# Decay rows through DRAM, one exponential for both masks, and squared norms of k from one-column products, in a hybrid decoder layer

## The reference

```python
kd = l2norm(heads(ck, DN_H))                       # k / sqrt(sum(k * k) + eps), per token and head
g = -jnp.exp(dn_a_log) * jax.nn.softplus(da + dn_dt_bias)
beta = jax.nn.sigmoid(db)
...
G = jnp.cumsum(gc, axis=-1)
diff = G[..., :, None] - G[..., None, :]
dec = jnp.where(incl, jnp.exp(jnp.where(incl, diff, 0.0)), 0.0)
kk = jnp.einsum('bhid,bhjd->bhij', kc, kc)
a_mat = jnp.where(strict, kk * dec * bc[..., :, None], 0.0)
eG = jnp.exp(G)[..., None]
...
qk = jnp.einsum('bhid,bhjd->bhij', qc, kc) * dec
```

## Time and profile before

| | us |
|---|---|
| median of 3 runs | 823.36 (823.05 to 825.56) |
| profiled execution, its time | 822.85 |
| its span in the profile | 821.0 |
| PE, busy | 802.8 |
| DVE, busy | 405.6 |
| ACT, busy | 214.8 |
| POOL, busy | 152.6 |

### The profile page before, as it was taken

One profiled execution on the slowest core, in us unless ns is written; L12 is line 12 of the kernel. 1 busy time (PEld: TensorE's weight loads), 2 busy tenths in 40 slices (PEclk: granted clock), 3 DMA queues, 4 the chain that ended last, 5 costly groups with the idle time before them and its releaser, 6 DMA issues. The chain is left out here.

```text
span 821.0 us, 12877 instructions
## 1 busy us (share of the span) xinstructions
PE 802.8 (98%) x5172; PEld 504.8 (61%) x5172; DVE 405.6 (49%) x886; ACT 214.8 (26%) x469; POOL 152.6 (19%) x182
## 2 busy tenths in 40 slices
PE   9999999999999999999999999999999999999995
PEld 4446777887889987777777776455433333334443
DVE  4223556684666522663853458826352101104976
ACT  3202152239324311131101110122121111125275
POOL 0324420004055223300220034000100001004100
PEclk9999999999999999999999999999999999999999
DMA  9521344503020200514241123134899999995211
GB/s 360 229 85 32 120 166 154 157 18 111 1 104 3 77 29 14 204 52 124 103 177 65 67 103 119 65 131 183 308 397 362 421 426 423 402 400 204 77 52 65
DMA packets 20977, 135.23 MB, mean 165 GB/s; under 512 B 2437, under 2 KB 3077, under 8 KB 13749
## 3 DMA queue, kind: packets, MB, share of 16 engines
q1 hardware_dynamic: 13328, 103.08, 32.1%
q0 software_dynamic: 4720, 23.83, 7.9%
q10 hardware_dynamic: 2868, 7.47, 3.0%
HBM read 118.94 MB, written 19.63 MB: 169 GB/s over the span
## 5 line engine op out<-in xcount | busy, mean ns | idle before, releaser
L818 PE MATMUL pair<-mem 128*128 128x288 f32 x640 | 158.9, 408 | 0.0
L818 PEld LDWEIGHTS pair<-mem 128*128 128x128 f32 x640 | 120.3, 190 | 35.6 <-ACT mem L1506 2.1
L986 PE MATMUL single<-mem 128*128 128x288 f32 x448 | 110.0, 407 | 0.2
L986 PEld LDWEIGHTS single<-mem 128*128 128x128 f32 x448 | 84.7, 190 | 25.7 <-issue 1.6
L1373 PE MATMUL single<-mem 128*32 128x512 f32 x768 | 85.1, 594 | 0.9 <-DVE mem L2539 0.9
L1506 ACT ACTIVATE mem<-pair 128x512 f32<-128x512 f32 (+5 forms) x83 | 36.5, 487 | 162.6 <-PE pair L818 63.1
L1506 ACT ACTIVATE mem<-single 128x256 f32<-128x256 f32 (+5 forms) x109 | 44.6, 419 | 126.9 <-PE single L1234 48.5
L2532 DVE SCALAR_TENSOR_TENSOR mem<-single,mem 128x256 f32<-128x256 f32 x12 | 5.8, 484 | 102.3 <-PE single L1373 91.4
L1373 PEld LDWEIGHTS single<-mem 128*32 128x32 f32 x768 | 23.6, 110 | 52.8 <-issue 51.7
L1225 PE MATMUL pair<-mem 128*128 128x512 f32 x112 | 51.0, 601 | 0.0
L1442 PE MATMUL pair<-mem 128*128 128x512 f32 x112 | 49.4, 595 | 0.3 <-DVE mem L2600 0.3
(11 more groups left out here) (431 smaller groups left out, 1118.1 us busy)
## 6 DMA issues: line engine op xcount, KB each, us to landing
mem<-in_w_gu SPq DMA_DIRECT2D x17, 2048.0 KB, 14.4
mem<-in_w_down SPq DMA_DIRECT2D x17, 1024.0 KB, 13.2
y_slots<-mem SPq DMA_DIRECT2D x9, 512.0 KB, 10.5
y_slots<-in_zeros POOLq DMA_DIRECT2D x8, 512.0 KB, 8.6
mem<-in_w_ga SPq DMA_DIRECT2D x2, 2048.0 KB, 7.7
mem<-in_w_gb SPq DMA_DIRECT2D x2, 2048.0 KB, 7.6
mem<-in_w_wo SPq DMA_DIRECT2D x2, 2048.0 KB, 7.7
mem<-in_w_pg SPq DMA_DIRECT2D x2, 2048.0 KB, 16.6
```

Source lines behind the costliest of these rows:

```text
L818: last = nc.tensor.matmul(pb[:, hf, 0:HALF], w(k), rhs[:, k, hf * HALF:(hf + 1) * HALF], start=(k == 0), stop=(k == kk - 1))
L986: last = nc.tensor.matmul(single[plan.buf[s]][:, 0:HALF], lhs[:, k, :], rhs[:, k, :], start=(k == 0 and j in (0, 1, 3, 4)), stop=(k == 3), ...
```

## The change

- `gG` is one step instead of five. PE makes the running sums of all tiles and heads as rows of 16 and of 4 partitions, with two products; DVE copies them to `grow`; ACT's queue writes them to DRAM (`g_rows`, two transfers).
- `gL`, new, after `nl` in block 6: ACT's queue reads each tile's four rows back to all 128 partitions (five transfers, into `Gr`).
- `gD` is gone. In `gE` ACT takes |G_j - G_i| with four absolute values (bias `gcum`, scale -1) into `D2`, one exponential with scale -1, and the one for `E`; POOL makes both masks out of `D2`, the one into `A` first. ACT waits for all five transfers before the first tile.
- `gs` is one step instead of five. POOL squares k in four products (`ksq`, in the buffers of `n_rows`, after the last `nf` and after the masks of tiles 0 and 1), PE multiplies tiles of the squares with one column of ones, DVE copies 20 columns out.
- The order: `gC` and `gG` from block 7 to block 4, ahead of `rN`; `gE` from blocks 9 and 10 to 7 (tiles 0, 1), 8, 9 and 10; `gs`, `gX` and `gr` in block 10.

```diff
     between = {2: [("nq", "rN", m) for m in (0, 1)], 3: [("nq", "rN", m) for m in (2, 3)],
-               4: [("rN",), ("nr", "rN")], 5: [("ns", "rN")], 6: [("nl", "rN")],
-               7: nf("rN", (0, 1)) + [("gC",), ("gG", 0), ("gG", 1), ("gD", 0), ("gD", 1)],
-               8: nf("rN", (2, 3)) + [("gG", t) for t in range(2, NT)] + [("gD", t) for t in range(2, NT)],
-               9: [("gs", t) for t in range(3)] + [("gE", 0), ("gE", 1)],
-               10: [("gs", 3), ("gs", 4)] + [("gE", t) for t in range(2, NT)] + [("gX",)], 11: [("gr",)]}
+               4: [("gC",), ("gG",), ("rN",), ("nr", "rN")], 5: [("ns", "rN")], 6: [("nl", "rN"), ("gL",)],
+               7: nf("rN", (0, 1)) + [("gE", 0), ("gE", 1)], 8: nf("rN", (2, 3)) + [("gE", 2)], 9: [("gE", 3)],
+               10: [("gs",), ("gE", 4), ("gX",), ("gr",)], 11: []}
...
+    g_rows = nc.dram_tensor("g_rows", (NT * H, P), F32, kind="Internal").ap()
...
-        ksq = [view(slot(14 + i), H, DK) for i in range(2)]
+        ksq = nrow["rN"]
...
                 elif k0 == "gG":
-                    t, n = s[1], ntok(s[1])
                     pe.wait_ge(sem("g_beta"), 1)
-                    out = heads(s, P, n)
-                    for h in range(H):
-                        last = nc.tensor.matmul(out[:, h, :], gl[0:n, t, h:h + 1].broadcast_to([n, P]), tri(t),
-                                                start=True, stop=True)
+                    out = single[plan.buf[s]]
+                    nc.tensor.matmul(out[0:16, 0:P], gl[:, 0:4, :], tri(0), start=True, stop=True)
+                    last = nc.tensor.matmul(out[32:32 + H, 0:64], gl[0:64, 4, :], tri(4), start=True, stop=True)
                     last.then_inc(s_mm, 1)
...
                 elif k0 == "gs":
-                    t, n = s[1], ntok(s[1])
-                    pe.wait_ge(sem("conv"), 8)
-                    out = single[plan.buf[s]][0:n, :].rearrange("p (h w) -> p h w", h=H)
-                    for h in range(H):
-                        last = nc.tensor.transpose(out[:, h, :], cs[:, 4 + h, t * P:t * P + n], C("ident"))
+                    pe.wait_ge(sem("ksq"), H)
+                    for t in range(NT):
+                        for h in range(H):
+                            at = H * t + h
+                            last = nc.tensor.matmul(single[plan.buf[s]][0:ntok(t), at:at + 1], ksq[h][:, t * P:t * P + ntok(t)],
+                                                    C("ones")[:, 0:1], start=True, stop=True)
                     last.then_inc(s_mm, 1)
...
-                elif k0 == "gs":
-                    t, n = s[1], ntok(s[1])
-                    mm_wait(act, s)
-                    if t >= 2:
-                        ev_wait(act, ("gs", t - 2))
-                    for h in range(H):
-                        last = nc.scalar.activation(ksq[t % 2][0:n, h, :], single[plan.buf[s]][0:n, h * DK:(h + 1) * DK], ACT.Square,
-                                                    accum_out=kr[0:n, 0, t, h:h + 1])
-                    last.then_inc(ev(k0), 1)
...
                 elif k0 == "gG":
-                    t, n = s[1], ntok(s[1])
-                    mm_wait(act, s)
+
+                    ev_wait(act, s)
+                    act.dma_start(g_rows[0:16, :], grow[0:16, :]).then_inc(sem("g_stored"), 16)
+                    act.dma_start(g_rows[16:20, 0:64], grow[32:36, 0:64]).then_inc(sem("g_stored"), 16)
+                elif k0 == "gL":
+
+                    act.wait_ge(sem("g_stored"), 32)
                     act.wait_ge(sem("ret_free"), 1)
-                    copy(Gr[t], heads(s, P, n)).then_inc(ev(k0), 1)
+                    for t in range(NT):
+                        n = ntok(t)
+                        act.dma_start(Gr[t], g_rows[4 * t:4 * t + 4, 0:n].unsqueeze(0).broadcast_to([P, H, n])).then_inc(sem("g_rows"), 16)
                 elif k0 == "gE":
                     t, n = s[1], ntok(s[1])
-                    act.wait_ge(sem("gdiff"), t + 1)
-                    nc.scalar.activation(A[t], A[t], ACT.Exp, scale=-1.0).then_inc(sem("gexp"), 1)
-                    nc.scalar.activation(D2[t], D2[t], ACT.Exp).then_inc(sem("gexp"), 1)
+                    ev_wait(act, ("gC",))
+                    act.wait_ge(sem("g_rows"), 16 * NT)
+                    for h in range(H):
+                        last = nc.scalar.activation(D2[t][:, h, :], Gr[t][0:n, h, :], ACT.Abs, bias=gcum[0:n, t, h:h + 1], scale=-1.0)
+                    link(last)
+                    nc.scalar.activation(D2[t], D2[t], ACT.Exp, scale=-1.0).then_inc(sem("gexp"), 1)
                     nc.scalar.activation(E[t], Gr[t], ACT.Exp).then_inc(sem("gexp"), 1)
...
-                elif k0 == "gD":
-                    t, n = s[1], ntok(s[1])
-                    ev_wait(dve, ("gG", t))
-                    for h in range(H):
-
-                        V.tensor_scalar(A[t][:, h, :], Gr[t][0:n, h, :], gcum[0:n, t, h:h + 1], 0.0, ALU.subtract, ALU.max)
-                        last = V.tensor_scalar(D2[t][:, h, :], Gr[t][0:n, h, :], gcum[0:n, t, h:h + 1], 0.0, ALU.subtract, ALU.min)
-                    last.then_inc(sem("gdiff"), 1)
+                elif k0 == "gG":
+                    mm_wait(dve, s)
+                    V.tensor_copy(grow[0:16, :], single[plan.buf[s]][0:16, 0:P])
+                    V.tensor_copy(grow[32:36, 0:64], single[plan.buf[s]][32:36, 0:64]).then_inc(ev(k0), 1)
+                elif k0 == "gs":
+                    mm_wait(dve, s)
+                    V.tensor_copy(kr[:, 0, 0:4], single[plan.buf[s]][:, 0:16].rearrange("p (t h) -> p t h", t=4))
+                    V.tensor_copy(kr[0:64, 0, 4], single[plan.buf[s]][0:64, 16:20]).then_inc(ev(k0), 1)
...
+                elif k0 == "nf" and s[1:] == ("rN", 3):
+
+                    pool.wait_ge(sem("nfin"), 4)
+                    for h in range(H):
+                        pool.wait_ge(sem("conv"), H + h + 1)
+                        G.tensor_tensor(ksq[h], cs[:, H + h, :], cs[:, H + h, :], ALU.mult).then_inc(sem("ksq"), 1)
                 elif k0 == "gE":
                     t, n = s[1], ntok(s[1])
                     if t == 0:
                         pool.wait_ge(sem("nfin"), 4)
                         G.memset(nwz, 0.0).then_inc(sem("zeroed"), 1)
-                    pool.wait_ge(sem("gexp"), 5 * t + 1)
-                    G.tensor_tensor(A[t], A[t], bh(C("low") if t < 4 else C("low_s", 64), n, n), ALU.mult).then_inc(sem("gmask"), 1)
-                    pool.wait_ge(sem("gexp"), 5 * t + 2)
+                    pool.wait_ge(sem("gexp"), 4 * t + 1)
+                    G.tensor_tensor(A[t], D2[t], bh(C("low") if t < 4 else C("low_s", 64), n, n), ALU.mult).then_inc(sem("gmask"), 1)
+                    pool.wait_ge(sem("gmask"), 2 * t + 1)
                     G.tensor_tensor(D2[t], D2[t], bh(tri(t), n, n), ALU.mult).then_inc(sem("gmask"), 1)
```

9 lines of the change are left out of this document (5 added, 4 removed).

## The result

| | before | after |
|---|---|---|
| median of 6 runs, us | 824.2 (822.82 to 825.94) | **836.24** (832.74 to 839.46) |
| ratio | | 1.0144, 95% interval 1.012 to 1.0168 |
| profiled execution, its time | 822.85 | 837.3 |
| its span | 821.0 | 835.5 |

The account below looks back on a forecast made before the run. PE was taken as the bound, busy 802.8 of 821.0 us. 822.85 + 4.1 (block 11 later) + 2.0 (clock) = 828.95; with the median 0.5 higher, 829.5 us, range 824 to 837.

Parts of the forecast that it names:

- PE's balance: PE's work in gG and gs: 6.98 us removed, 0.5 and 4.3 added, 2.2 us less.
- one column is nearly free: Rival on gs: its one-column products cost at most 1.0 us instead of 4.3, no difference in time; chance 0.03.
- Step 1, shift: On PE, gC and gG ahead of rN delay block 7 by 1.26 us; block 10 ends at 182.7.
- Step 2, arrival: The five g_rows transfers from DRAM have all landed at 167 us, between a floor of 162.9 and a ceiling of 170.9.
- w_dz goes first: Rival on the transfers: rows land at 172, with short pieces costing 1 us; about 835.5 us; chance 0.13.
- in time: Rival on the transfers: rows land by 161.7, result 822.2 us, not slower; chance 0.22 for in time or nearly.
- Step 3, ACT: On ACT, gE of tiles 0 and 1 takes 5.7 us after the rows arrive, before block 8's evacuation.
- Step 4, DVE: From block 8's evacuation through convolution and two nf to the release of POOL's memset: 5.96 us.
- Step 5, POOL: POOL's memset, four masks and four squares of k (ksq) ahead of gs take 10.45 us.
- The wait: PE, ready for gs at 182.7, stands 6.4 us until POOL's squares are done at 189.1.
- The clock: The granted clock may fall during PE's standing, slowing gs and part of block 11: 2.0 us taken, at most 12.
- the clock holds: Rival on PE's clock after its standing: no fall, 827.5 us; counted within the forecast's 0.57, without its own chance.

Follow-up runs that it names:

- e12: The changed kernel with rows of tiles 0 and 1 on their own semaphore and POOL squaring k ahead of memset and first masks; 823.78 us, ratio 0.9998 to before.
- e1: The changed kernel with the exponentials (gE) one block later in the order; 823.83 us, ratio 1.0011 to the kernel before.
- e4: The changed kernel with 16 useless products on PE ahead of gs's wait; 831.78 us, ratio 1.0101 to the kernel before.
- e13: e1 with 128 columns of ones in each product of squares instead of one; 822.56 us, ratio 0.9994 to the kernel before.
- e5: The changed kernel with POOL squaring k ahead of the memset and the masks of tiles 0 and 1; 829.18 us, ratio 1.0056 to the kernel before.
- e6: The changed kernel with ACT waiting for the transfers of tiles 0 and 1 alone, on their own semaphore; 831.44 us, ratio 1.009 to the kernel before.
- e9: e1 with 24 columns of ones in each product of squares instead of one; 824.52 us, ratio 1.0003 to the kernel before.
- e2: The kernel before with only the squares of k changed (POOL squares, PE's one-column products), decay rows as they were; 829.82 us, ratio 1.0062.
- e7: The changed kernel with gs and gr after block 11 instead of block 10; 825.28 us, ratio 1.0031 to the kernel before.
- e8: e1 with gs split, tiles 0 and 1 after block 10 and the rest after block 11; 823.9 us, ratio 0.9996 to the kernel before.
- e3: The changed kernel with the norms of k as before (transposes, ACT's Squares) and the exponentials late; 820.39 us, ratio 0.9966 to the kernel before.

## Why the prediction was right in direction and short in size

The mechanism came true: the rows hold ACT, ACT holds DVE, DVE holds POOL, and PE stands for POOL's squares. What failed are sizes in the sum: the term for the clock, 2.0, measured 5.35; the wait, 6.4, measured 8.56; and the pause of 1.44 behind had no term.

**One sum fits the runs with products of squares.** At full clock and without a wait the changed stretch is 71.14 - 4.80 - 2.18 + 0.53 + 4.11 = 68.80. Add each run's waits and half of the time that PE worked at half clock: e12 68.80 + 1.7 = 70.5 (70.49 measured), e1 + 3.4 = 72.2 (72.01), e4 + 7.76 + 1.7 = 78.3 (78.25), e13 + 0.57 = 69.4 (69.37), e5 + 3.81 + 5.1 = 77.7 (77.94), e6 + 4.44 + 6.05 = 79.3 (79.19), the change + 8.56 + 5.35 = 82.7 (82.69).

- *PE's balance*, -2.2: right. 68.80 against 71.14 is -2.3. The price of the one-column products, 4.3, taken from the weights of the nearest row, measured 4.11. The rival "one column is nearly free" is dead: 4.11/40 is 0.103 us a record. The floor of 25 ns that the Trainium skill states ("TensorE: Matmul & The Clock Gate", section "Wait — 56ns, not 53.3ns?") doesn't carry over to products that load new weights each. Here the weights set the pace: in e9 the 40 weight loads take 4.36 us, one behind the other, and 24 columns cost what one does (4.15 against 4.11).
- *Step 1, shift*: right. Block 10 ended at 184.92, less the late start 182.95, against 182.7.
- *Step 2, arrival*: 167 forecast; 169.72 - 1.97 = 167.75. Right, on the row taken as nearest; "w_dz goes first" (172) and "in time" (162) did not occur. The transfers landed 6.9 to 9.0 us after their issue. That it varies by 3.3 us from run to run wasn't in the forecast. It may be part of the changed kernel's spread (832.74 to 839.46); that isn't shown.
- *Step 3, ACT*: 5.7 forecast, 6.37 measured. Four absolute values take 1.3 us, not 0.8 and a 0.2 wait.
- *Step 4, DVE*: 5.96 forecast, 5.94 measured.
- *Step 5, POOL*: 10.45 forecast, 11.30 measured. The masks took 5.04 for the first four (4.4 forecast) and the squares 5.35 (5.03); beside what, see the last section.
- *The wait*: 6.4 forecast, 8.56 measured; 0.75 + 0.67 + 0.85 from steps 2, 3 and 5 make the 2.2.
- *The clock*: the step that failed most. "I take 2.0, half of gs" measured 5.35. The forecast's own numbers spoke against half: a fall 4.9 us after PE stops is at 187.6, PE was to come back at 189.1, so the whole of gs, 4.3, stood behind the fall. Measured, it fell 2.2 us into the wait, at 187.1, which is before PE came back all the same, so the moment isn't what made the term small. The rise is: it came at 204.2, after 10.7 us of PE's work. gs took 7.83 instead of 4.11, and the two blocks behind it 17.03 instead of 15.52. Wrong too was the idea that only standing costs clock: with the wait filled (e4) 3.65 of the 5.35 are gone and 1.7 stay, and behind the products of squares the clock stood at half for 3.4 or 6.8 us in e1, e2, e4, e7, e8, e9 and e12, where PE had stood for 0.16 us at most. The Trainium skill says of the gate that it follows how busy PE has been recently ("TensorE: Matmul & The Clock Gate", section "Part 1: The HAM clock gate"). The busy time of the profile doesn't show the fall coming: e1's window has PE busy 5.00 of 5.00 us at a mean clock of 0.53.
- *Outside the stretch*: +4.1 and +2.0 were all that I charged. The pause of 1.44 us at the dense products was missing. The late start of 1.97 is in the profiled execution and isn't the change's; the forecast, which starts from one execution's time, can't have it.
- *What is hidden*: right. The blocks 5 to 10 run in 46.9 us without a gap, so ACT's lost Squares, DVE's lost gD, the square root behind the new copies and the early table loads cost nothing.
- *The signs*: the gap before the one-column products, ended by L2837; ACT's idle ended by the rows; the clock under 1 after 187: all there. POOL's memset came at 182.03, 180.1 without the late start, against 178.7. "One-column records at 0.11" held only in the runs at full clock. PE makes nothing up behind: its dense products begin at 252.51, 13.5 us later than before.

The stretch was forecast at 71.14 + 4.1 + 2.0 = 77.24; of the 5.45 missing 2.2 are wait and 3.35 clock, less 0.2 of price. The rival "the clock holds" is dead too: with these products it didn't hold even where PE had no wait.

## What to carry to other kernels

Before a step is moved earlier, look at what stands behind it on its queue: ACT waited for rows that it could have used a block later, and two convolutions, one memset and PE stood behind it. A product costs its weights, so replacing 20 transposes by 20 products with one column doubled PE's bill (2.18 us, then 4.11), and behind them the clock stood at half for 3.4 us or more in every kernel that has them, with or without a wait. Split a change by its halves before judging it: here one half gains 0.34% (0.53% with PE's program padded; the two intervals overlap) and the other loses 0.62%.

## What the hardware did that I had not expected

- The granted clock fell with PE busy all the time: 2.5 us after the first one-column product in e1 (6.8 us at half), for 3.4 us with 24 columns (e9), not at all with 128 (e13) nor with the transposes (e3).
- In the profiled executions a shorter wait didn't cost less clock: 4.44 us of standing (e6) brought 13.7 us at half, of which PE worked in 12.1, more than the 10.7 behind the wait of 8.56. Over all executions the mean granted clock is 0.9905 in e6 (4) and 0.9875 with the change (6).
- PE pauses at a fixed place of its program in dense products: 0.9 to 2.5 us in the variants that have it, moved by 8 records with 16 instructions and gone with 80. What PE does in it, the fetching of instructions or something else, stays open.
- DVE and POOL slow one another. In e6 the same instruction of DVE before POOL starts and beside it:

```profile
173.47 0.75 DVE L2049 SCALAR_TENSOR_TENSOR mem<-mem,vec 128x512 f32<-128x512 f32 x1
...
181.93 1.54 DVE L2049 SCALAR_TENSOR_TENSOR mem<-mem,vec 128x512 f32<-128x512 f32 x1
```

And POOL's same four squares took 4.46 us with DVE busy for 1.88 of them (e1), 4.64 with 3.35 (e5 and e12), 5.35 with 5.28 (the change and e7, PE standing in the one and working in the other). No run changes only this, so that it is why POOL's steps took 11.3 us instead of 10.45 is likely, not shown.
